# Softmax branch of a mixer layer: probabilities scaled on ScalarE, values as the stationary operand, two transposes moved later

## What is computed

```
x = x + MixerBlock(RMSNorm(x));  x = x + HierMoE(RMSNorm(x))
```

```
logits = jnp.where(valid[:, None], logits, -jnp.inf)
p = jax.nn.softmax(logits, axis=-1).astype(v.dtype)
return jnp.einsum('bhqk,bqkhd->bqhd', p, v_sel)
...
merged = gates[:, :, 0] * (branches[0] @ w_branch[0])
```

## Time and profile before

| | |
|---|---|
| median of three runs | 874.33 us |
| profiled execution | 876.39 us, of it span 874.6 us |
| TensorE matmuls | 813.4 us busy, 93% of the span |
| VectorE | 529.7 us, 61% |
| ScalarE | 383.4 us, 44% |
| GpSimd | 119.7 us, 14% |
| DMA | mean 322 GB/s |
| mean granted TensorE clock | 0.974 of full speed |

### The profile page before, as it was taken

The page is one execution under the profiler, slowest core; times in us unless marked ns, Lnnn a source line. Parts: engine busy times, 40 slices in busy tenths (PEclk is TensorE's granted clock), DMA queues, the critical chain, the costliest instruction groups (busy, mean ns, idle before and its releaser), DMA issues.

```text
span 874.6 us, 20283 instructions
## 1 busy us (share of the span) xinstructions
PE 813.4 (93%) x8723; PEld 646.8 (74%) x8723; DVE 529.7 (61%) x1071; ACT 383.4 (44%) x653; POOL 119.7 (14%) x169
## 2 busy tenths in 40 slices
PE   7999999999999998976899999999999999986884
PEld 7898778878887765654589978787889776663652
DVE  5778898658555554433376788976656455543434
ACT  5546877545422222111275678764444222211113
POOL 2740102212000000000056001023200000000000
PEclk9999999999999999889999999999999999999988
DMA  9966554499979999999998464555997999999994
GB/s 307 389 233 154 185 170 168 144 395 382 378 299 420 419 418 420 420 420 421 399 374 290 153 223 129 174 192 205 421 375 276 416 420 419 420 419 420 420 419 167
DMA packets 65277, 281.47 MB, mean 322 GB/s; under 512 B 5248, under 2 KB 7376, under 8 KB 41888
## 3 DMA queue, kind: packets, MB, share of 16 engines
q1 hardware_dynamic: 63904, 278.45, 81.6%
q0 software_dynamic: 800, 1.40, 1.1%
q10 hardware_dynamic: 480, 0.28, 0.1%
HBM read 279.06 MB, written 1.05 MB: 320 GB/s over the span
## 4 chain that ended last, share of the span: by engine, by line
PE 73%; DMA 18%; SPq 6%; DVE 2%; issue 1%; ACT 1%; DVEq 0%; ACTq 0%
PE ps L512 15%; PE ps L514 14%; PE ps L513 14%; PE ps L875 9%; DMA ring<-in_w_exp_up 7%; DMA late<-in_w_exp_down 6%; PE ps L859 5%; PE ps L891 4%; SPq L388 3%; DMA late<-in_w_exp_up 3%; PE ps L976 3%; SPq L412 2%; DMA ring<-in_w_in 2%; PE ps L881 1%; PE ps L810 1%
## 5 line engine op out<-in xcount | busy, mean ns | idle before, releaser
L1725 DVE TENSOR_TENSOR split_lo<-ring,split_hi 128x1024 fp32r<-128x1024 f32 (+1 forms) x142 | 198.1, 1432 | 33.2 <-ACT split_hi L1201 32.3
L512 PE MATMUL ps<-split_hi,hT_hi 128*128 128x512 f32 (+2 forms) x416 | 161.5, 388 | 2.0 <-DVE split_lo L1725 1.0
L1201 ACT ACTIVATE split_hi<-ring 128x1024 fp32r<-128x1024 f32 (+1 forms) x144 | 145.9, 1049 | 33.3 <-PE ps L514 31.0
L513 PE MATMUL ps<-split_lo,hT_hi 128*128 128x512 f32 (+2 forms) x416 | 157.6, 379 | 0.0
L514 PE MATMUL ps<-split_hi,hT_lo 128*128 128x512 f32 (+2 forms) x384 | 145.2, 378 | 0.0
L2152 DVE TENSOR_TENSOR wsT<-mb,ps 32x64 f32<-32x64 f32 x256 | 54.9, 214 | 141.3 <-ACT mb L1407 138.7
L1407 ACT ACTIVATE mb<-ps 128x64 f32<-128x64 f32 x64 | 14.3, 224 | 236.2 <-PE ps L875 236.2
L512 PEld LDWEIGHTS ps<-split_hi,hT_hi 128*128 128x128 f32 x416 | 78.1, 188 | 20.7 <-issue 4.7
L513 PEld LDWEIGHTS ps<-split_lo,hT_hi 128*128 128x128 f32 x416 | 78.3, 188 | 12.8
L514 PEld LDWEIGHTS ps<-split_hi,hT_lo 128*128 128x128 f32 x384 | 72.2, 188 | 13.3
L1629 POOL TENSOR_TENSOR idx<-idx,wt 128x128 f32<-128x128 f32 x32 | 12.2, 401 | 383.1 <-PE ps L897 304.8
(11 more groups left out here) (282 smaller groups left out, 1293.8 us busy)
## 6 DMA issues: line engine op xcount, KB each, us to landing
ring<-in_w_in SPq DMA_DIRECT2D x52, 1024.0 KB, 8.9
ring<-in_w_exp_gate SPq DMA_DIRECT2D x43, 1024.0 KB, 23.6
ring<-in_w_exp_up SPq DMA_DIRECT2D x43, 1024.0 KB, 26.6
late<-in_w_exp_down SPq DMA_DIRECT2D x38, 1024.0 KB, 26.1
ring<-in_w_exp_down SPq DMA_DIRECT2D x15, 1024.0 KB, 27.9
late<-in_w_exp_gate SPq DMA_DIRECT2D x9, 1024.0 KB, 25.4
late<-in_w_exp_up SPq DMA_DIRECT2D x9, 1024.0 KB, 27.5
ring<-in_w_branch SPq DMA_DIRECT2D x8, 1024.0 KB, 4.8
```

Of the source, the lines that this page charges most:

```text
L512: mm(dst, st[0], mv[0], start=start, stop=False, skip_group_check=True)
L513: mm(dst, st[0], mv[1], start=False, stop=False, skip_group_check=True)
L1201: A(half_view(split_hi[:, v % SPLITS, :], v), raw_half(v, l), ACT.Copy).then_inc(hi_done, 1)
L1725: V.tensor_tensor(half_view(split_lo[:, v % SPLITS, :], v), raw_half(v, l), half_view(split_hi[:, v % SPLITS, :], v).bitcast(F32), ALU.sub ...
```

## The change

The exponentials are multiplied by one over their sums in place, on ScalarE, before they are transposed (`scale_probabilities`, for each tile four copies with a scale per partition). The sums' reciprocals of both tiles are taken on VectorE as soon as the sums are there. The product is `pv_turned` for both tiles, both written into bank 7 side by side, and `yT_high` and `yT_low` read that bank. `y_evac_a` and `y_transposes(y_ab, 6)` are gone. On TensorE the first transposes come one unit later, the second ones one unit later, the second product one unit later.

```diff
@@ TensorE
-                    def pv(v, t, b0):
...
                     in_unit(20, 13)
-                    pe.wait_ge(*L(la_exp, 1))
+                    in_unit(21, 13)
+                    pe.wait_ge(*L(p_scaled, 1))
                     p_transposes(sc, 0, 6)
-                    in_unit(21, 13)
+                    wide_unit(22, 14, y_tile(0), True, True)
                     pe.wait_ge(*L(pT_out, 3))
-                    pv(vi, 0, 7)
-                    pe.wait_ge(*L(la_exp, 2))
+                    pv_turned(vi, 0, 7)
+                    pe.wait_ge(*L(p_scaled, 2))
                     p_transposes(zc, 1, 4)
-                    wide_unit(22, 14, y_tile(0), True, True)
                     in_unit(23, 16)
+                    in_unit(24, 16)
                     pe.wait_ge(*L(pT_out, 4))
-                    pe.wait_ge(*L(y_out, 1))
-                    pv(vi, 1, 7)
-                    in_unit(24, 16)
-                    pe.wait_ge(*L(y_out, 2))
-                    y_transposes(y_ab, 6)
+                    pv_turned(vi, 1, 7)
                     in_unit(25, 17)
@@ SyncE, buffer yy for an expert's corner
-                            sp.wait_ge(*L(yT_mm, 2))
+                            sp.wait_ge(*L(pv_mm, 4))
@@ ScalarE
+                    def scale_probabilities(t, p):
+
+                        act.wait_ge(*L(inv_ok, t + 1))
+                        for s_ in range(NH):
+                            inv = inv_of[t][:, s_:s_ + 1]
+                            ins = A(p[:, s_, 0:P * t + P], p[:, s_, 0:P * t + P], ACT.Copy, scale=inv)
+                        ins.then_inc(p_scaled, 1)
...
                     hi(22)
+                    scale_probabilities(0, sc)
+                    scale_probabilities(1, zc)
                     p_evac(3, 0, 6)
...
-                    yT_high(L(yT_mm, 2), 1, 6)
+                    yT_high(L(pv_mm, 4), 1, 7)
@@ GpSimd
-                    pool.wait_ge(*L(yT_mm, 2))
+                    pool.wait_ge(*L(pv_mm, 4))
@@ VectorE
-                            link(V.reciprocal(scal[:, 52:56], lsum))
+                            V.reciprocal(inv_of[0], lsum).then_inc(inv_ok, 1)
+                            dve.wait_ge(*L(inv_ok, 1))
...
-                    def y_evac_a(t):
...
+                    def second_sums():
+                        dve.wait_ge(*L(la_exp, 2))
+                        V.reciprocal(inv_of[1], lsum).then_inc(inv_ok, 1)
...
                     lo(21)
+                    second_sums()
                     lo(22)
-                    y_evac_a(0)
                     gate(3, 13)
...
-                    y_evac_a(1)
                     gate(4, 16)
                     lo(26)
-                    yT_low(4, 1, 6)
+                    yT_low(4, 1, 7)
```

More of the change, by code:

```diff
@@ L104 @@
     ws_T=1, ws_ready=1, block_out=22, rot_i=2, rot_a=2, idx_T=1, idx_out=1, rel_mm=1, rel_out=2,
-    qk_T=1, qk_out=1, zc_mm=2, zc_out=2, zabs=4, zln=2, zarg=2, zexp=2, pT_mm=4, pT_out=4, pv_mm=4, y_out=2,
-    conv_y=1, ln_var=1, ln_root=1, vn_dve=1, vn_done=1, sgu_mm=1, yb_done=1, yT_mm=2, yT_hi_out=4, yT_lo_out=4,
+    qk_T=1, qk_out=1, zc_mm=2, zc_out=2, zabs=4, zln=2, zarg=2, zexp=2, pT_mm=4, pT_out=4, pv_mm=4, inv_ok=2, p_scaled=2,
+    conv_y=1, ln_var=1, ln_root=1, vn_dve=1, vn_done=1, sgu_mm=1, yb_done=1, yT_mm=1, yT_hi_out=4, yT_lo_out=4,
     la_mm=2, la_max=2, la_exp=2, gate_prod=8, gate_sum=6, mid_mm=2, wide_mm=4, x_mid=3,
@@ L250, in build @@
             sem("zc_mm"), sem("zc_out"), sem("zabs"), sem("zln"), sem("zarg"))
-        zexp, pT_mm, pT_out, pv_mm, y_out = (
-            sem("zexp"), sem("pT_mm"), sem("pT_out"), sem("pv_mm"), sem("y_out"))
+        zexp, pT_mm, pT_out, pv_mm, inv_ok, p_scaled = (
+            sem("zexp"), sem("pT_mm"), sem("pT_out"), sem("pv_mm"), sem("inv_ok"), sem("p_scaled"))
         conv_y, ln_var, ln_root, vn_dve, vn_done = (
@@ L428, in build @@
         top8 = scal[:, 16:24]
+        inv_of = (scal[:, 52:56], scal[:, 16:20])
         lmax, lneg, lsum, linv = (scal[:, 24 + 4 * i:28 + 4 * i] for i in range(4))
```

## The result

| | before | after |
|---|---|---|
| median | 874.46 us (4 runs) | 887.79 us (4 runs, 886.31 to 888.39) |
| ratio | | 1.0145, interval 1.0132 to 1.0158 |
| profiled execution, span | 876.39, 874.6 us | 886.31, 884.5 us |
| mean granted clock | 0.974 | 0.967 |

What follows compares the result with a forecast made beforehand. It took TensorE, busy 93% of the span, as the bound. Per layer -1.2 + 0.36 + 2.1 + 2.4, say +3.6 us, so +7.2 us for two layers, gave 881.5 us; range 879.2 to 885.6.

Steps and rivals of the forecast that it cites:

- Where the loss comes from: In each layer TensorE would stand inside wide_unit(22) and ahead of unit 23, waiting for ScalarE: 2.1 and 2.4 us.
- First wait: After wide_unit(22)'s sixth matmul, TensorE waits for token_evac(13), queued behind p_evac(3): loss 2.1 us a layer, bounds 1.7 and 2.5.
- second: Ahead of unit 23, TensorE waits for block_evac(14), queued behind p_evac(4): loss 2.4 us a layer, bounds 2.1 and 2.6.
- Product of tile 1: The turned product for tile 1 on TensorE would take 1.02 us in place of 1.70 us.
- of tile 0: The turned product for tile 0 on TensorE would take 0.6 us in place of 0.84 us.
- Net, without falls: All terms of one layer together, with the clock left out: +3.65, say +3.6 us.
- Transposes moved behind unit 21: The first transposes gain nothing by leaving their old place and cost 0.36 us a layer in the open behind unit 21.
- Scaling hidden: ScalarE's eight scaling copies ahead of p_evac(3) would take 2.8 us under a cover of 3.7 us, costing nothing.
- The loss reaches the end: A late mixer moves the whole stream of experts' loads, so each layer's loss passes in full into the total time.
- The clock kept out of the sum: Clock falls behind the two pauses were counted as nothing, since full units lie ahead of and behind them.
- second rival: Both waits, and the clock falls: 1.7 us a fall; 883.2 us for one, 888.3 for four; 20 in 100.
- The first rival: No new wait, both evacuations free when wanted: 2.4 us faster at 871.9 us with the transposes hidden; 4 in 100.

Runs made afterwards that it cites:

- e4: The changed kernel with ScalarE's two copies, p_evac(3) and p_evac(4), moved behind the evacuations TensorE waits for; 875.28 us, 1.0005 of before.
- e5: The kernel before with TensorE's moves alone, VectorE's first division later, values still moving, nothing scaled on ScalarE; 887.40 us, 1.0138 of before.
- e1: The changed kernel with 8 and 10 matmuls on constants filling TensorE's two new pauses in each layer; 881.62 us, 1.0076 of before.
- e12: The changed kernel itself, nothing altered, in a second execution with a profile; 883.74 us.
- e6: The changed kernel without its moves: scaling and turned product kept, TensorE's order as before, ScalarE's scaling placed to suit; 871.13 us, 0.9954 of before.
- e7: The changed kernel with 4 and 5 matmuls on constants in the two pauses, half as many as e1; 882.44 us, 1.0081 of before.

## Why the prediction was right and wrong, by its own steps
- **Where the loss comes from: right.** Both new waits came with the engine, the instruction and the place that were named, in both layers; e4 takes the second away and halves the first by ScalarE's order alone, and e5 shows the moves alone to be enough.
- **Their sizes: right.** First wait 2.05 us for 2.1, second 2.47 for 2.4. Product of tile 1 1.03 us for 1.02, of tile 0 0.59 for 0.6. Net, without falls, 3.7 us a layer (e1, and layer 0 of e12) for 3.6.
- **Transposes moved behind unit 21: right.** From the end of unit 20 to the end of unit 21 it takes as long as before, since the second half still waits for its low part (the row at 142.73), and 0.36 us come on top behind the unit.
- **Scaling hidden: right.** 2.86 us for the 2.8 taken, ready 0.84 us early.
- **A slip without weight.** The stretch of 26.6 us from unit 21's transposes to unit 25 holds four units (21 to 24), not five; no term of the sum uses it.
- **The loss reaches the end: right.** e1 has 3.7 us a layer in the timeline and 6.5 us in the time. In the change, the stream of the experts' loads still runs dry ahead of the experts' first slots, 5 us later than in the earlier trace rows (the columns are those of that group):

```profile
245.00:250.00 5.00, 4.90 (x64) 4.69 (x67) 3.62 (x17) 2.86 (x4) 0.76 (x2) 1.00 0.40 161
```

- **The clock kept out of the sum: this step failed.** The sum put the clock at nothing; the falls are worth 6.8 us by e1, where the forecast missed by 6.3. The prediction had the price (1.7 us a fall) and, in its second rival, the outcome for four falls, 888.3 us. It gave that rival 20 in 100, on two grounds. One was a single row where a pause of 2.9 us among the experts did no harm. The other was that full units around a pause would hold the clock up. The runs refute the second: among full units 7 of 8 pauses of 2.5 us lowered it. The first was one draw of something that varies: the first pause of layer 0 of the change, with the same length and the same work around it, ended in a fall in one execution and without one in the other (e12). A rival with a known price and a chance per pause should have been priced with that chance four times over. With the counts over all kernels, 2 x 4/12 + 2 x 7/8 = 2.4 falls are to be expected in an execution, 4.1 us on top of 881.5, so 885.6; with those of the change alone, 6 falls in two executions, it is 5.1 us, 886.6. Both lie below the measured 887.8. The falls in the three executions without a profile are not known, and the one with all four falls was the fastest of the four, at 886.31 us: that the median comes so near to the 888.3 of four falls is in part luck.
- **The rule that was cited.** The Trainium skill, "TensorE: Matmul & The Clock Gate", section "A second HAM failure mode: psum-queue depth-cycling", says of another kernel that TensorE micro-idles between groups of matmuls frequently enough for the clock to go back and forth, each time at a cost. The trace after agrees on the going back and forth and on the cost, four times at 1.7 us; but here it took single pauses of 2 us, and those of 1.0 to 1.2 us did nothing in 8 cases. The prediction cited the rule and went by the row against it.
- **The first rival** (no new wait, 871.9 us) is near what e6 reaches in another way, at 871.1 us: a gain was there, and the moves gave it away. That the two numbers are so close is luck, as 1.6 us of e6's gain have no account.

## What to carry to other kernels
Before an operation is moved on one engine's list, write down what follows its consumer on the other engine's list: a copy that waits for late transposes holds up every evacuation behind it, and the cure is to order that engine by when each result is wanted (e4), or not to move at all (e6). A pause of TensorE of some 2 us in a dense stretch is to be priced at its length plus a share of a clock fall; where it can't be removed, a few matmuls on constants that cut it to 1 us save that share (e7, no fall in four pauses). If busy time rises while instructions get fewer, look at the clock by windows before looking for another wait.

## What the runs showed of the hardware
A fall of the clock cost 1.6 to 1.7 us each time in the mixers. Among the experts it was not always so short: in the trace of before TensorE was busy from 350 to 355 us with the clock at 0.50, in the last microsecond 0.54, which cost 0.50 x 4 + 0.46 = 2.5 us. The length of a pause alone does not settle whether one follows: 0 of 8 at 1.0 to 1.2 us, 4 of 12 at 2.05, 7 of 8 at 2.47, with the same pause in the same place of the same kernel ending either way. Lengths between 1.2 and 2.05 us did not occur, and what part the work around a pause has was not tested by itself. A switch of ScalarE's table, straight behind a copy, took 1.28 us, and the evacuation started 0.02 us after it.
